# First output tile prepared inside the unit stage, no barrier at its end, convolution state stored by DMA, recurrence samples moved to the convolution slots

## The reference

```
h = RMSNorm(x) * g_pre;  p = h @ w_in          # 1024 -> 3344 columns, split among the groups
A: u = c_c * c_x; out = c_b * conv3(u) * silu(c_z); new_conv = last 2 rows of u
B: gated linear attention, 4 heads of 64:  S_t = diag(a_t) S_{t-1} + k_t^T v_t, o_t = q_t S_t,
   RMSNorm per head, * silu(z)
C: sliding window attention (window 128, 4 query and 2 key heads, rotary, sinks) * silu(z)
D: attention over 256 memory tokens * silu(z)
x = x + RMSNorm(concat(A, B, C, D) @ w_out) * g_post
```

## Time and profile before

| | us |
|---|---|
| median of 3 runs | 2118.95 |
| the runs | 2116.91 to 2126.06 |
| the profiled execution | 2123.05 |
| its span, first to last instruction | 2120.9 |
| PE busy in it | 1978.8 (93%) |
| DVE busy | 1276.0 (60%) |
| ACT busy | 880.4 (42%) |
| POOL busy | 332.2 (16%) |

### The profile page before, as it was taken

The page is one execution under the profiler, slowest core; times in us unless marked ns, Lnnn a source line. Parts: engine busy times, 40 slices in busy tenths (PEclk is TensorE's granted clock), DMA queues, the critical chain, the costliest instruction groups (busy, mean ns, idle before and its releaser), DMA issues. The chain is left out here.

```text
span 2120.9 us, 42798 instructions
## 1 busy us (share of the span) xinstructions
PE 1978.8 (93%) x16314; PEld 1121.9 (53%) x16314; DVE 1276.0 (60%) x2845; ACT 880.4 (42%) x2175; POOL 332.2 (16%) x251
## 2 busy tenths in 40 slices
PE   9999899989999998898999997998999999889998
PEld 4455444444566665565544544443546666555633
DVE  5577765665356755555646786566645676645533
ACT  4554343543444332343445543344435452332322
POOL 1444323000000000000124343320100000000000
PEclk9999999999999999999999998999999999999999
DMA  7732244656521133354365232546563113234532
GB/s 263 179 99 57 66 120 120 149 171 205 132 57 32 51 84 88 95 132 150 136 160 137 70 85 66 144 117 180 167 194 71 62 52 74 51 96 106 139 113 89
DMA packets 327495, 241.66 MB, mean 114 GB/s; under 512 B 188631, under 2 KB 273117, under 8 KB 327261
## 3 DMA queue, kind: packets, MB, share of 16 engines
q1 hardware_dynamic: 324180, 228.34, 39.4%
q10 hardware_dynamic: 3112, 10.59, 1.6%
HBM read 136.60 MB, written 57.71 MB: 92 GB/s over the span
## 5 line engine op out<-in xcount | busy, mean ns | idle before, releaser
L2021 PE MATMUL bank<-h_hi,w_parts 128*128 128x512 f16 (+4 forms) x4240 | 837.9, 344 | 40.4 <-ACTq L2409 17.3
L2021 PEld LDWEIGHTS bank<-h_hi,w_parts 128*128 128x128 f16 (+1 forms) x4240 | 401.5, 98 | 392.9 <-issue 86.5
L2021 PE MATMUL bank<-h_lo,w_parts 128*128 128x512 f16 (+3 forms) x2160 | 439.5, 345 | 0.8
L2021 PEld LDWEIGHTS bank<-h_lo,w_parts 128*128 128x128 f16 (+1 forms) x2160 | 206.9, 98 | 180.0 <-issue 16.7
L3147 PE MATMUL bank<-scr_h,tb_h 128*128 128x512 f16 x768 | 179.3, 393 | 15.0 <-ACT tb_h L2431 9.9
L3147 PE MATMUL bank<-w_parts,tb_h 128*128 128x512 f16 x768 | 170.3, 379 | 1.6 <-DVEq L3295 1.6
L2408 ACT ACTIVATE tb<-bank 128x512 f32<-128x512 f32 (+1 forms) x140 | 71.9, 514 | 224.8 <-PE bank L2021 210.1
L2977 POOL TENSOR_SCALAR w_raw<-w_raw 128x1024 f32<-128x1024 f32 x46 | 132.3, 2883 | 76.8 <-DMA w_raw<-in_w_in 76.1
L2543 ACT ACTIVATE bank<-bank,stat 128x256 f32<-128x256 f32 x256 | 113.7, 446 | 58.7 <-DVE stat L2906 58.4
L3147 PEld LDWEIGHTS bank<-scr_h,tb_h 128*128 128x128 f16 x768 | 76.8, 101 | 109.0 <-issue 15.0
L2972 POOL TENSOR_TENSOR w_parts<-w_raw,w_parts 128x1024 f16<-128x1024 f32 x46 | 101.4, 2207 | 206.1 <-ACT w_parts L2381 205.3
(11 more groups left out here) (339 smaller groups left out, 2718.3 us busy)
## 6 DMA issues: line engine op xcount, KB each, us to landing
w_in_kept<-w_parts SPq DMA_DIRECT2D x104, 256.0 KB, 3.1
w_parts<-w_in_kept SPq DMA_DIRECT2D x104, 256.0 KB, 2.9
w_raw<-in_w_in SPq DMA_DIRECT2D x48, 512.0 KB, 4.3
out<-scr SPq DMA_DIRECT2D x32, 512.0 KB, 2.6
scr<-in_x_prompt SPq DMA_DIRECT2D x16, 512.0 KB, 4.1
scr<-out SPq DMA_DIRECT2D x16, 512.0 KB, 4.2
rot<-out ACTq DMA_DIRECT2D x12, 512.0 KB, 3.8
mix_t<-in_x_prompt SPq DMA_DIRECT2D x8, 512.0 KB, 11.7
```

Of the source, the lines that this page charges most:

```text
L2021: m = mm(bank[b][0:m_w, 0:c1 - c0], w[:, k, 0:m_w], h[:, k, c0:c1], start=it["piece"] == 0 and k == 0, stop=it["piece"] == 2 and k == KT - 1)
```

## The change

- B0s and B1s are done beside A0's steps 0 and 1 (slots 8 and 9). `SAMPLE_ROW` gives A0s buffer 0, C1s buffer 1 and D1s buffer 2. Buffer 0's user before A0s is C0s, of slot 7.
- Step 1 of C is joined in second passes too. A slot of A is joined where nothing but A is in it: slots 8, 9, 14 and 15 in first passes, 14 and 15 in second ones.
- `conv_out` is no longer an item of PE and ACT. It is emitted right behind the last eviction of x, for each A step but step 0, and SP stores 128 channels of the state by a DMA whose destination runs along channels: one element of 4 bytes at a time, 256 of them for a prompt and 2048 for a sample step. Each counts as one store of `stored`.
- `o_mix` is placed once slot 12 has ended and A1's step 0 is gated, and waits for the end of slot 12 and that gate.
- The last slot's end on PE is like the others. The waits for banks move into the output stage: banks 2 and 3 before the first product, 4 to 7 and `left["pe"]` behind it. ACT waits for PE's last end before it signals `left["act"]`, and no longer for `left["pe"]` before tile 1.
- The output stage begins: prepare output tile 1, normalize x tile 0, product (0, half 0), normalize x tile 1, late splits, product (1, half 0), turn h tiles 0 and 1, normalize x tile 2, product (0, half 1).

```diff
-SAMPLE_ROW = {("D", 0): 0, ("B", 0): 1, ("B", 1): 2, ("C", 0): 0, ("A", 0): 1, ("C", 1): 0, ("D", 1): 1, ("A", 1): 0}
+SAMPLE_ROW = {("D", 0): 0, ("B", 0): 1, ("B", 1): 2, ("C", 0): 0, ("A", 0): 0, ("C", 1): 1, ("D", 1): 2, ("A", 1): 0}
...
-            main = ("C", st["g"], 0) if st["unit"] == "B" else (st["unit"], st["g"], 1)
+            main = ("A", 0, st["g"]) if st["unit"] == "B" else (st["unit"], st["g"], 1)
...
-        return s["st"] == 1 and (s["unit"] == "D" or s["unit"] == "C" and not with_sample)
+        return s["st"] == 1 and s["unit"] in "CD"
...
+        if with_sample and (ev["unit"], ev["role"]) == ("A", "x") and ev["last"]:
+            for st in groups[ev["group"]]:
+                if st["st"] != 0:
+                    emit(item("conv_out", step=st))
...
+        if not mixed[0] and ended >= len(slots) - 3 and ("evict", slots[-2]["main"]["n"], "z") in placed:
+            emit(item("o_mix"))
+            mixed[0] = True
...
-            if ended == len(slots) - 1:
-                emit(item("o_mix"))
...
-                main.append(item("begin", slot=x["index"], steps=[x["main"]] + x["side"], joined=False))
+                free = x["main"]["unit"] == "A" and all(s["unit"] == "A" for s in x["side"])
+                main.append(item("begin", slot=x["index"], steps=[x["main"]] + x["side"], joined=free))
...
+                elif it["kind"] == "conv_out":
+
+                    s = it["step"]
+                    g, sample = s["g"], s["st"] == "s"
+                    sp.wait_ge(u_done, conv_steps.index(s["n"]) + 1)
+                    dst = of_layer((conv_s if sample else conv_p).rearrange("l b t d -> l (b t) d"), l)[:, P * g:P * g + P]
+                    sp.dma_start(dst.rearrange("t p -> p t"), conv_st_t[:, g] if sample else conv_tail[:, g]).then_inc(stored, 16)
...
-                    if it["slot"] == n_slots - 1:
-
-                        for b in range(2, 8):
-                            pe.wait_ge(bank_free[b], plan["uses"][b])
-                        pe.drain().then_inc(left["pe"], 1)
-                    else:
-                        pe.drain().then_inc(step_pe, 1)
-                elif kind == "conv_out":
...
+                    pe.drain().then_inc(step_pe, 1)
...
+                    if it["slot"] == n_slots - 1:
+
+                        act.wait_ge(step_pe, n_slots)
...
-                    all_steps_done(act, n_slots - 1)
+                    all_steps_done(act, n_slots - 3)
+                    gate_written(act, next(x["n"] for x in plan["steps"] if (x["unit"], x["g"], x["st"]) == ("A", 1, 0)))
...
-        order = [("xn", 0), ("mix", 1), ("o", 0, 0), ("h", 0), ("xn", 1)] + [("split", i) for i in late]
-        order += [("o", 1, 0), ("h", 1), ("xn", 2), ("o", 0, 1), ("fin", 0), ("mix", 2), ("o", 1, 1), ("h", 2), ("xn", 3), ("fin", 1), ("mix", 3)]
+        first_o = ("o", 0, 0)
+        order = [("mix", 1), ("xn", 0), ("o", 0, 0), ("xn", 1)] + [("split", i) for i in late] + [("o", 1, 0), ("h", 0), ("h", 1)]
+        order += [ ("xn", 2), ("o", 0, 1), ("fin", 0), ("mix", 2), ("o", 1, 1), ("h", 2), ("xn", 3), ("fin", 1), ("mix", 3)]
...
+                    if x == first_o:
+
+                        for b in range(4, 8):
+                            pe.wait_ge(bank_free[b], plan["uses"][b])
+                        pe.drain().then_inc(left["pe"], 1)
```

More of the change, by code:

```diff
@@ L394, in place @@
             run("PE", 0.9 if unit == "C" else 1.1, self.needs(it))
-        elif k in ("conv_out", "swa_out", "conv_in", "layer_in"):
+        elif k == "conv_out":
+            self.issue(2, when(("conv", n)))
+        elif k in ("swa_out", "conv_in", "layer_in"):
             p = run("PE", 0.4, self.needs(it))
@@ L413 @@
 ON_PE = ("proj", "gate", "rope_k", "cache_t", "score", "turn", "value", "value_part", "gla_p", "gla_t", "gla_kv", "gla_s",
-         "gla_o", "gla_sq", "gla_norm", "conv_out", "swa_out")
+         "gla_o", "gla_sq", "gla_norm", "swa_out")
 STATS = 4
@@ L440, in last_reader @@
             return ("evict", n, "z"), u
-        return ("conv_out", n, 0) if with_sample and u["st"] != 0 else ("evict", n, "x"), u
+        return ("evict", n, "x"), u
     reader = {"B": dict(q=("gla_p", n, end), k=("gla_p", n, end), v=("gla_t", n, end - 1), z=("gla_norm", n, 0)),
@@ L531, in work @@
         if kind == "A":
-            if with_sample and st != 0:
-                out.append(item("conv_out", [2], step=s))
-        elif kind == "B":
+            return out
+        if kind == "B":
             chunks = 1 if sample else ST // CH
@@ L599, in plan_units @@
     n_kept = [0]
+    mixed = [False]
     last_on_pe = [None]
@@ L1252, in stores_of @@
         if it["kind"] == "conv_out":
-            return int(it["step"]["g"] == 1)
+            return 1
         if it["kind"] == "gla_sq":
@@ L1469, in units @@
         lr = low[0:2 * RANK + 1]
-        out_c = low[64:80, 0:4 * P].rearrange("p (i g n) -> p i g n", i=2, g=2)
         o, _ = STAGE["in"]
@@ L1638, in units @@
         for it in items:
-            if it["kind"] in ("score", "turn", "value", "gla_p", "gla_t", "gla_o", "gla_sq", "rope_k", "conv_out"):
+            if it["kind"] in ("score", "turn", "value", "gla_p", "gla_t", "gla_o", "gla_sq", "rope_k"):
                 att_uses[(it["kind"], it["step"]["n"], it.get("c", 0))] = it["banks"]
@@ L2428, in on_scalar @@
                 elif kind == "o_mix":
-                    all_steps_done(act, n_slots - 1)
+                    all_steps_done(act, n_slots - 3)
+                    gate_written(act, next(x["n"] for x in plan["steps"] if (x["unit"], x["g"], x["st"]) == ("A", 1, 0)))
                     fn(m_hi[:, 0], mix_t[:, :, 0:P], ACT.Copy, scale=M_UP).then_inc(mh_done, 1)
-                elif kind == "conv_out":
-                    s = it["step"]
-                    i = 1 if s["st"] == "s" else 0
-                    rows = 2 * NB if i else 2
-                    filled(act, it, 2)
-                    link(fn(out_c[0:rows, i, s["g"], :], bank[2][0:rows, 0:P], ACT.Copy))
-                    act.drain().then_inc(bank_free[2], 1)
-                    if s["g"] == 1:
-                        dst = conv_s if i else conv_p
-                        act.dma_start(of_layer(dst.rearrange("l b t d -> l (b t) d"), l),
-                                      out_c[0:rows, i].rearrange("p g n -> p (g n)")).then_inc(stored, 16)
                 elif kind == "gate":
@@ L3123, in on_tensor @@
         def on_tensor(pe):
-            for x in order:
+            for i, x in enumerate(order):
                 if x[0] == "o":
@@ L3127, in on_tensor @@
                     b = out_bank(t, n)
+                    if x == first_o:
+                        for b in range(2, 4):
+                            pe.wait_ge(bank_free[b], plan["uses"][b])
+                        b = out_bank(t, n)
                     if t >= 2:
@@ L3186, in on_scalar @@
                     if t == 1:
-                        for e in ("pe", "dve"):
-                            act.wait_ge(left[e], no)
+                        act.wait_ge(left["dve"], no)
                     if t >= 2:
-                        act.wait_ge(out_full[out_bank(t, 1)], t // 2)
+                        for n in range(2):
+                            act.wait_ge(out_full[out_bank(t, n)], t // 2)
                     fn(m_hi[:, t % 2, :, 0:out_size(t)], mix_t[:, :, tcols(tile_at[t])], ACT.Copy, scale=M_UP).then_inc(mh_done, 1)
@@ L3233, in on_vector @@
             n_root = n_low = 0
-            if build is not None:
-                dve.wait_ge(pre_in, 16)
-                link(ts(pre_g, pre_g, H_UP, None, ALU.mult))
             for x in order:
@@ L3240, in on_vector @@
                     r = size(u)
+                    if u == 0:
+                        dve.wait_ge(pre_in, 16)
+                        link(ts(pre_g, pre_g, H_UP, None, ALU.mult))
                     z = st_h[0:r, u % 2]
@@ L3255, in on_vector @@
                     if t >= 2:
-                        dve.wait_ge(out_full[out_bank(t, 1)], t // 2)
+                        for n in range(2):
+                            dve.wait_ge(out_full[out_bank(t, n)], t // 2)
                     m_low = m_lo[:, t % 2] if r == P else m_hi[:, t % 2, :, r:2 * r]
```

14 lines of the change are left out of this document (2 added, 12 removed).

## The result

| | before | after |
|---|---|---|
| median of the runs | 2119.15 us (2116.91 to 2126.06, 4 runs) | 2143.27 us (2138.05 to 2148.24, 4 runs) |
| profiled execution | 2123.05 | 2142.48 |
| its span | 2120.9 | 2140.7 |

What follows compares the result with a forecast made beforehand. PE (busy 93% of the span) and its holes were taken as the bound. Second passes gain 9.6 us each (19.2), first passes 9.6 together: 28.8, giving 2094 from 2123.05 or 2090 from the median; forecast 2092 us, range 2072 to 2120.

Steps and rivals of the forecast that it cites:

- State by DMA: Second passes: SP's element-wise state stores could delay D11's transposes, 0.5 us a pass lost (bounds 0 and 4); PE gains 0.3.
- The DMA rival: 4-byte stores hold up SP's weights, key copies and transposes; PE sees some 5 us at each of four: 2110, chance 0.06.
- B samples out of the C slots: Second passes, the main term: B samples moved beside A0, 10.3 us gained a pass.
- The slot-6 holes: Second passes, tail of B0s in slot 6: PE's 3.39, 1.36 and 1.35 us without work go, 6.1 us gained.
- C10's wait for its query: Second passes: without B1s in front on DVE, the query is ready long before; 3.0 us a pass gained, bounds 0 and 3.0.
- the projections' waits on DVE's evictions of x: Second passes, A0's x and b evictions (7.4 us in two passes): half goes, 1.8 a pass gained, bounds -1 and 3.7.
- The clock term: Second passes, 801 to 806, behind the slot-6 hole: PE's low clock there goes too, 1.8 us gained.
- C0s blocks the projections: Rival: end of slot 7 in second passes, a hole up to 17.5 us and 3 at low clock: slower, 2136; chance 0.13.
- Barriers of slots 8 and 9: First passes: joined slots don't wait on PE's own ends; 3.6 us gained in all, bounds 0 and 3.8.
- End of the unit stage: Output tile 0 prepared early: 3.0 us a first pass gained, 6.0 for two (bounds 1.4 and 8.5 a pass).
- `o_mix`: Placed within D1's softmax, delays the last value products: 0.7 us lost a first pass, 0.5 a second, bounds 0 and 2.3.
- the 3.7 a first pass at product (0, half 1): First passes' output stage: product (0, half 1) starts at 448.3, not 451.99, 3.7 us gained.

Runs made afterwards that it cites:

- e1: The changed kernel with the convolution state stored as in the kernel before (transposed on PE, evicted by ACT, one contiguous DMA): 2088.70 us.
- e2: The kernel before with only the convolution state's element-by-element stores by DMA from SP added: 2175.68 us.
- e3: The changed kernel with the same element-wise stores issued by ACT in its own queue, not by SP: 2137.05 us.
- e9: The changed kernel with the samples' 2048 elements of 4 bytes written 512 bytes apart to a scratch tensor, that output left out: 2095.91 us.
- e6: e1 with the B samples back in the C slots, their buffers and the barrier before C's step 1 in second passes as before: 2118.10 us.
- e8: The kernel before with only the B samples moved, their buffers and C's joined step; A slots not joined, output mixed late, contiguous stores: 2088.97 us.
- e7: e1 with a barrier at every A slot (A slots not joined): 2094.06 us.
- e12: e8 with the A slots joined in first passes alone: 2088.64 us.
- e5: e1 with the old output stage, `o_mix` after the last slot as in the kernel before: 2083.80 us.
- e15: e1 with `o_mix` after the last slot in every pass, the output stage's new order kept: 2081.30 us.
- e11: The changed kernel with only half (1024 of 2048) of the elements of each samples' store written: 2121.76 us.
- e4: The changed kernel without the samples' state stores; the prompt's stores of 256 elements stay: 2089.66 us.
- e10: The changed kernel with the samples' state written to a scratch tensor as 128 contiguous pieces of 64 bytes, that output left out: 2088.68 us.

## Why the prediction was wrong

- **State by DMA is the step that failed.** I gave it 0.5 us a pass with a bound of 4, less 0.3 for the transposes that PE loses; it costs 27 a pass, 54.6 in the two second passes (e1; 55.7 in e2). I named the right place (the transposes of D11's probabilities behind A1's store) and took the size from two nearest rows, both of them *loads*, and from the time of the *issue*. The issue is 0.39 us. What counts is how long the writes keep the DMAs behind them from landing, 15 to 20 us, and no load shows that. An unknown whose nearest rows are of another direction needed a far wider bound than 4, and with it a wider range.
- **The DMA rival** had the mechanism and its sign: delays by the small stores, seen as waits on transposes behind a store. Its 5 us a store seen by PE was well under half of the 13.7 measured, and it put the cause in SP's queue; e3 has its stores in ACT's, and SP is held all the same. Of the page that I cited (the Trainium skill, "DMA: Bandwidth & Descriptors", "Rules for kernel authors"), one descriptor per element agrees with the trace: 9307 more packets of under 512 B, for 8192 + 1024 elements. The Trainium skill's rule on the same page, in "Specifications", that short writes are read-modify-writes doesn't size the cost: e9's 4-byte writes are as short, and cost 7.2 us where the same writes side by side cost 54.6. No run here shows whether the chip reads before it writes.
- **B samples out of the C slots** went as forecast, and more: 10.3 a pass forecast, 14.7 measured (29.4, e1 and e6; 30.0 for e8), for the moved samples, the buffers and the joined C together, which is also what my term held. The slot-6 holes and C10's wait for its query are gone, the projections' waits on DVE's evictions of x fall from 7.4 to 3.4, and slot 7 of e1 ends with holes of at most 0.7 us in one second pass and 1.4 in the other. The clock term was wrong: from 801 to 806 e1 still has a granted clock of 0.63 for 0.60 in the earlier trace rows; small holes at the end of the joined pair (PE is busy 3.57 of the 5 us from 796 to 801) came before it, where the kernel before had the large one.
- **C0s blocks the projections** is refuted: no hole of over 2 us at the end of slot 7, neither in the changed kernel nor in e1.
- **Barriers of slots 8 and 9**: 3.6 forecast. The four waits on PE's own end (3.8) are gone from e1's trace and stand in e7's (3.7). But the 5.2 and 5.4 measured are for joining every A slot, those of A1 in all passes too, and joined in first passes alone they bring 0.3 (e12 against e8, runs that overlap). So the price of this term isn't confirmed.
- **End of the unit stage** had the wrong sign. Forecast 6.0 gained in first passes and 1.0 lost in second ones; the square shows 5 lost. Its parts in the timeline were seen right (10.80 for the two products, waits of 3 and 1.3 forecast, 2.85 and 1.21 measured). Two terms were wrong. `o_mix`, at 0.7 and 0.5 a pass, costs 7.4 in four passes, and that is what is left after the products' earlier start: in the place looked at, 1.06 us of ACT and 1.23 of DVE stand ahead of an eviction and so stop PE's projections. And the 3.7 a first pass at product (0, half 1) is not gained: counted from the pass's first projection it starts at 402.0 and 400.3 in e1, 400.6 and 403.5 with the old output (e5), 400.9 and 401.5 with tile 0 late (e15); in the kernel before, whose A slots aren't joined, it is 403.7 and 407.4. What the products start earlier is given back at the h tiles.

Without the stores, and with the transposes that they replaced, the sum was 29.2 (28.8 + 1.0 - 0.6), and e1 measures 31.3 against the runs beside it. That is luck: 10 us too little for the samples and the barriers cancel 10 too much for the output.

## What to carry to other kernels

A DMA that scatters 4-byte elements side by side into DRAM is not free because its issue is short: ask what must land within the next 20 us, and write contiguous runs in place of it (64 bytes were enough here). If the trace has no row for an operation in the same direction and form, the nearest row bounds nothing: ask what the kernel loses if the delay is several times as long, and widen the range by that. Work moved forward off a wait is paid on the engines that it lands on: look at which evictions stand behind it, and at what is late next, before you count the wait as gained.

## What the runs showed of the hardware

- Element-wise stores of 2048 x 4 bytes to neighbouring addresses: 13.7 us of kernel time a store (e1), and 15 us with a DMA share of 0.6 to 1.35 at 10 to 16 GB/s; half of them 8.3 (e11); 256 elements none that shows (e4); 512 bytes apart 1.8, with 5 us at 12 GB/s (e9); packed in 64-byte pieces none (e10).
- The backlog is shared over queues (e3): two transposes take SP 12.65 us to issue behind stores that ACT issued, 6.40 in e1.
- Of the 12.2 us of PE at B's state products (L2133, "issue") behind A0's store, the two largest holes, 4.48 and 5.06, lie inside groups of matmuls between which the program waits for nothing. The holes at this place are smaller in e3 (4.7) and e11 (6.0) and gone in e1, e4, e9 and e10. Which of PE's needs the backlog delayed there, the profile doesn't show.
- The same instructions of two second passes took 3.9 us more or less, of 1070, in two executions (e8, e12).
